# A two-layer hybrid decoder step: high-half products first in the first pair of split up units, and two small vector steps placed behind the normalization

## The reference, cut to what matters

```
u_a, q_b, ... = split(x @ w_in)                     # 20 output tiles of 128
... xr[:, -1], xi[:, -1]                            # S5: last states of the prompt, an output
mix = concat(ya, yb, yc) @ w_out                    # 8 tiles
x = layer_norm(ALPHA * x + mix)
h  = x @ w_up                                       # 44 tiles, called up units here
hp = concat([prev, h])                              # prev: 2 earlier rows of each sample
c  = conv_b + sum(conv_w[j] * hp[:, j:j+L] for j in range(3))
a, gate = split(c)
x = layer_norm(ALPHA * x + (silu(gate) * a) @ w_down)
return x, (..., s5 last states, ..., hp[:, -2:])
```

## Time and profile before

| | |
|---|---|
| time, median of 3 runs | 678.52 us (678.46 to 678.6) |
| profiled execution, its own time | 678.88 us |
| its span | 677.1 us |
| TensorE busy (matmuls) | 666.4 us, 98% of the span |
| VectorE busy | 567.3 us, 84% |
| ScalarE busy | 417.5 us, 62% |
| GpSimd busy | 86.0 us, 13% |
| chain of waits that ended last | 83% TensorE, 11% VectorE, 2% ScalarE |

### The profile page before, as it was taken

One profiled execution on the slowest core, in us unless ns is written; L12 is line 12 of the kernel. 1 busy time (PEld: TensorE's weight loads), 2 busy tenths in 40 slices (PEclk: granted clock), 3 DMA queues, 4 the chain that ended last, 5 costly groups with the idle time before them and its releaser, 6 DMA issues.

```text
span 677.1 us, 13606 instructions
## 1 busy us (share of the span) xinstructions
PE 666.4 (98%) x5142; PEld 618.3 (91%) x5142; DVE 567.3 (84%) x1191; ACT 417.5 (62%) x684; POOL 86.0 (13%) x82
## 2 busy tenths in 40 slices
PE   9999999999999999999999999999999999999997
PEld 7777887989999999999976787999899999999996
DVE  6999998989998988789489998688899898884653
ACT  5776258758676666646747535687767666663343
POOL 0000000050222222200200000005012222220001
PEclk9999999999999999999999999999999999999999
DMA  8766620746574655554356563164666545555411
GB/s 321 245 262 219 192 89 5 265 117 227 201 256 151 204 182 183 198 187 153 128 180 226 164 205 127 63 239 143 176 212 214 188 158 192 183 190 195 157 62 65
DMA packets 42244, 120.65 MB, mean 178 GB/s; under 512 B 5378, under 2 KB 14754, under 8 KB 41666
## 3 DMA queue, kind: packets, MB, share of 16 engines
q1 hardware_dynamic: 40466, 115.22, 50.8%
q0 software_dynamic: 704, 3.06, 2.0%
q10 hardware_dynamic: 1008, 1.50, 0.6%
HBM read 114.28 MB, written 5.48 MB: 177 GB/s over the span
## 4 chain that ended last, share of the span: by engine, by line
PE 83%; DVE 11%; ACT 2%; DMA 1%; issue 1%; SPq 0%; DVEq 0%
PE ps L432 21%; PE ps L433 21%; PE ps L434 21%; PE ps L425 10%; DVE z L1452 2%; DVE z L1460 1%; DMA z<-in_xT 1%; PE ps L496 1%; PE ps L559 1%; PE ps L599 1%; PE ps L680 1%; PE ps L765 1%; PE ps L686 1%; PE ps L574 1%; DMA ring<-in_units 1%
## 5 line engine op out<-in xcount | busy, mean ns | idle before, releaser
L1548 DVE TENSOR_TENSOR w_lo<-ring,w_hi 128x1024 fp32r<-128x1024 f32 x144 | 175.7, 1222 | 38.4 <-ACT w_hi L954 36.7
L432 PE MATMUL ps<-x_hi,w_hi 128*128 128x264 f32 x672 | 191.2, 284 | 1.0 <-DVE x_lo L1498 1.0
L433 PE MATMUL ps<-x_lo,w_hi 128*128 128x264 f32 x672 | 190.6, 284 | 0.0
L434 PE MATMUL ps<-x_hi,w_lo 128*128 128x264 f32 x672 | 190.5, 284 | 0.0
L954 ACT CAST w_hi<-ring 128x1024 fp32r<-128x1024 f32 x144 | 150.3, 1044 | 62.6 <-PE ps L434 59.8
L432 PEld LDWEIGHTS ps<-x_hi,w_hi 128*128 128x128 f32 x672 | 126.7, 189 | 1.9 <-issue 1.8
L433 PEld LDWEIGHTS ps<-x_lo,w_hi 128*128 128x128 f32 x672 | 126.7, 189 | 0.0
L434 PEld LDWEIGHTS ps<-x_hi,w_lo 128*128 128x128 f32 x672 | 126.1, 188 | 0.0
L425 PE MATMUL ps<-x,ring 128*128 128x264 f32 x480 | 112.0, 390 | 0.1
L425 PEld LDWEIGHTS ps<-x,ring 128*128 128x128 f32 x480 | 89.3, 190 | 18.7 <-issue 2.2
L432 PE MATMUL ps<-hff_hi,w_hi 128*128 128x264 f32 x352 | 100.1, 284 | 0.0
(11 more groups left out here) (348 smaller groups left out, 1094.0 us busy)
## 6 DMA issues: line engine op xcount, KB each, us to landing
ring<-in_units SPq DMA_DIRECT2D x187, 512.0 KB, 3.6
kv<-in_kpool SPq DMA_DIRECT2D x32, 128.0 KB, 2.4
kv<-in_vpool SPq DMA_DIRECT2D x32, 128.0 KB, 2.5
SR<-in_sret SPq DMA_DIRECT2D x2, 1024.0 KB, 5.9
out_rsample<-SR POOLq DMA_DIRECT2D x2, 1024.0 KB, 5.1
out_kv<-hb ACTq DMA_DIRECT2D x2, 528.0 KB, 4.7
out_y<-x SPq DMA_DIRECT2D x3, 264.0 KB, 2.1
prev<-in_prev SPq DMA_DIRECT2D x2, 352.0 KB, 5.0
```

Of the source, the lines that this page charges most:

```text
L432: mm(out, wh, hi, start=start, stop=False)
L433: mm(out, wh, lo, start=False, stop=False)
L434: return mm(out, wl, hi, start=False, stop=stop)
L1548: E.did(tt(w_lo[:, slot], ring[:, ring_slot(L * UNITS + i)], w_hi[:, slot].bitcast(F32), ALU.subtract), "w_lo")
```

## The change

In the pair of up units 2 and 3, TensorE waits for tile k of x_hi and does the two products with x_hi for both units; then it waits for tile k of x_lo and does the third product for both. The number of products is the same. `conv_prev` and `s5_finals` move from the attention part to behind `ln_tail_up`, before the loop over the convolutions, in this order and in both layers. GpSimd's store of `s5o` moves behind its additions of squares.

```diff
@@ tensor engine
                 for k in range(KT):
-                    pe.wait_ge(S("x_lo"), x_count(L, k + 1))
+                    pe.wait_ge(S("x_hi"), x_count(L, k + 1))
                     for i, out in zip(pair, outs):
                         if k == 0:
                             wait_low(pe, L, UP + i)
-                        ins = split_product(out, UP + i, k, x_hi[:, k], x_lo[:, k], k == 0, k == KT - 1)
+                        mm(out, w_hi[:, split_slot(UP + i), k], x_hi[:, k], start=(k == 0), stop=False)
+                        mm(out, w_lo[:, split_slot(UP + i), k], x_hi[:, k], start=False, stop=False)
+                    pe.wait_ge(S("x_lo"), x_count(L, k + 1))
+                    for i, out in zip(pair, outs):
+                        ins = mm(out, w_hi[:, split_slot(UP + i), k], x_lo[:, k], start=False, stop=(k == KT - 1))
                         if k == KT - 1:
                             E.did(ins, "used")
@@ vector engine
                 s5_out(L)
-                s5_finals(L)
                 if EARLY[L]:
                     split_lo_early(L, EARLY[L][0])
                 sb_out(L)
                 if EARLY[L]:
                     lower_early(L, 1)
-                conv_prev(L)
...
                 ln_tail_up(L)
+                conv_prev(L)
+                s5_finals(L)
 
                 for i in range(N_UP):
@@ gpsimd
-                need(pool, "s5st", L, 1)
-                pool.dma_start(O["s5"][L], s5o[:]).then_inc(S("st_s5"), 16)
                 need(pool, "sr", L, 1)
                 pool.dma_start(O["rsample"][L], SR[:]).then_inc(S("st_sr"), 16)
                 ln_squares(2 * L + 1)
+                need(pool, "s5st", L, 1)
+                pool.dma_start(O["s5"][L], s5o[:]).then_inc(S("st_s5"), 16)
                 need(pool, "spre", L, 1)
                 pool.dma_start(O["convprev"][L], prev[:, :, 1]).then_inc(S("st_prev"), 16)
```

## The result

The changed kernel takes 681.24 us (median of 7 runs, 680.61 to 681.96). The kernel before took 678.61 us in the same measurement (678.46 to 678.83). The ratio is 1.0038, with a 95% interval from 1.0029 to 1.0047: slower by 0.38%, or 2.6 us. The forecast was 681.3 us. The profiled execution has a span of 680.1 us, 3.0 us more than before's.

The account below looks back on a forecast made before the run. TensorE was taken as the bound, with VectorE's splits nearly as much the limit. Product order and attention part add nothing, unit 6's stall 2 x 1.40 = 2.8 us: span 679.9, time 681.3 us, range 680.3 to 682.2 (8 in 10).

Parts of the forecast that it names:

- What bounds it: Whole kernel: TensorE is busy 98% of the span; VectorE's low halves lead it by only 0.34, 0.22 and 0.73 us.
- The pair: Up units 2 and 3: the new product order gains 0.48 us, of which 0 to 0.22 are left at unit 5.
- The attention part: Taking 2.03 us of VectorE work out of each layer there gains 0; the bound is all 2.03 us.
- The stall at unit 6: Up unit 6: its split comes late behind the moved steps, so TensorE waits 1.40 us a layer, 2.8 in all.
- GpSimd: GpSimd's queue: the later stores of s5o and prev end by 167 us, ahead of the down units' subtraction; cost 0.
- Rival 4: Behind the norm: GpSimd slows VectorE's convolution and split by 0.5 us a layer at most; 682.3 us, chance 5%.
- The sum: Whole kernel: span 677.1 + 2.8 = 679.9 us, time 681.3 us, 0.41% slower.
- rival 1: Up unit 6: VectorE has more room, unit 6 doesn't wait and the product order's gain holds; 677.6 us, chance 5%.
- rivals 2 and 3: Attention part: freed time counts, in one layer (679.3 us, chance 4%) or both with a small stall (676.9 us, 2%).

## Why the prediction was right, step by step

- **What bounds it.** No engine's busy time or clock changed, and 2.6 us were added all the same. The trace of before had no wait for a split, and the slack read from it was the right thing to read.
- **The pair.** The start was put at 152.27 us; it is 152.36, with 0.08 us of it from ahead of the norm's rate. The gain at the pair's end was put at 0.48 us; it is 0.49 in the order alone. The gain at unit 5 was put at 0 to 0.22 us; it is 0.11. Shown by the order alone: no change in the time. One step was slightly off: I expected a wait near 0.2 us behind the first 4 products. There the load at 153.06 us is only 0.11 us late, and it starts 0.05 us after x_lo tile 0 is ready, at about 152.58 + 0.43 = 153.01 (the 0.43 is the prediction's), not 0.23. The larger wait stands at tile 2 (154.76 us).
- **The attention part.** Put at 0, and leaving the steps out changed the time by nothing that can be told, 0.7 us at most.
- **The stall at unit 6.** Slack 0.73, moved work 2.03, delay 1.30 to 1.53, taken 1.40 us a layer. Measured 1.40 and 1.41. TensorE starts 0.11 us after the split's end, taken as 0.1; so the slack that counts is 0.73 - 0.11 = 0.62 us. The single moves bracket it: 0.60 us gives no delay, 1.43 gives 0.84.
- **GpSimd.** Cost 0, and moving the stores away shows 0. Rival 4 had the right neighbours and the wrong instruction: the store holds a copy, not the convolution's sums or the split.
- **The sum.** 2.8 us forecast; spans differ by 3.0, medians by 2.6. That the forecast of 681.3 us lies within 0.1 of the measured 681.24 is in part luck: the kernel before was 0.09 us slower in this measurement than in the one that the forecast starts from.

Rivals 1, 2 and 3 each fall by a run: rival 1 by the wait in the moves alone, rivals 2 and 3, which need 2.0 us or more from the attention part, by the steps left out, where at most 0.7 us are possible.

## What to carry to other kernels

Where an in-order engine feeds the bottleneck, no wait in the profile doesn't mean room: subtract the producer's end from the consumer's start at each hand-over, less what the hand-over itself takes (0.11 us here), and put in no more than the smallest difference behind that place. An earlier start of the bottleneck is worth only what the next hand-over lets through; here the reordering by itself gave no measurable change, and together with a gap some 10 us upstream, filled with one of the late splits, it gave 0.9 us. And when a step moves, look at what its stores will lie beside: the held copy, with the low clock that followed, decided over 4.8 us between two places of the same stores.

## What the runs showed of the hardware

- A small copy on VectorE ends only when GpSimd has issued its store: 1.62 us instead of 0.17 under a store of 2.10, ending with it in both layers, and 0.17 again with the store elsewhere. In the changed kernel the copy is caught at the end of the store, 0.48 us. The split that runs under the same store takes 1.22 us as always. The Trainium skill, page SBUF — State Buffer, section Who interferes with whom, says that the two engines share a port pair, that it goes to whoever issues first for its whole instruction, and that a copy can take it, under conditions on its operands. That an instruction with two inputs doesn't collide with the writing of descriptors, it gives as inferred. The trace agrees on both, with 1.62 and 1.22 us. That the ports are the reason is the page's account; the runs show only that the delay comes and goes with the store. I had read the earlier trace rows for the split alone and hadn't asked about the copy.
- After a wait of 2.01 us TensorE's granted clock fell to 0.50, about 1 us into the next unit, and stayed there for 3.3 us. After the wait of 1.46 us in the changed kernel the clock stayed full. So a longer stall can cost 1.5 us more than itself. Perhaps it need not: one of the five runs was 1.8 us faster than the others, at a higher mean clock. The Trainium skill, page TensorE: Matmul & The Clock Gate, section What's actually happening, describes the gate with the same two levels; no run here shows where between 1.46 and 2.01 us of waiting it sets in, or whether it is the wait's length alone.
- Where TensorE waits for a split, its first weight load starts 0.11 to 0.12 us after the split's recorded end.
- Left open: in the first layer the norm starts some tenths earlier or later from kernel to kernel (its mark lies between 146.94 and 148.38 us), ahead of all that was edited there, and the 0.36 us with which one profile ran late.
